# The last attention and the final norm of a two-block model, rescheduled on one core

## The reference

```python
proj = h @ w_in + b_in                      # h = rmsnorm(x, norm_c); q, k, v, g
logits = q k^T * scale - slope[head] * dist # 16 heads of 64, window 128, 2 kv heads
p = softmax([logits, sink])[..., :-1]       # dist >= 0 and dist < 128
o = p v
x = x + (o * silu(g)) @ w_out
return rmsnorm(x, final_norm)               # rows of 1024, one per token
```

## Time and profile before

| | us |
|---|---|
| median of 3 runs (1839.79 to 1842.37) | 1840.81 |
| the profiled execution | 1845.26 |
| its span | 1843.5 |
| from the start of the scores of head 0 to the start of the head loop's steady state | 1647.35 to 1668 |
| last values matmul to the eviction of the first residual tile | 1767.7 to 1784.96 |
| last residual tile taken out to the end | 1823.04 to 1843.5 |

### The profile page before, as it was taken

The page is one execution under the profiler, slowest core; times in us unless marked ns, Lnnn a source line. Parts: engine busy times, 40 slices in busy tenths (PEclk is TensorE's granted clock), DMA queues, the critical chain, the costliest instruction groups (busy, mean ns, idle before and its releaser), DMA issues.

```text
span 1843.5 us, 24067 instructions
## 1 busy us (share of the span) xinstructions
PE 1673.8 (91%) x8860; PEld 1412.3 (77%) x8860; DVE 1060.7 (58%) x1760; ACT 823.3 (45%) x1544; POOL 93.4 (5%) x112
## 2 busy tenths in 40 slices
PE   7998999998999999989999998889987979979977
PEld 6886787886778888868798896668765758859965
DVE  5557877674545656552254438864465984446654
ACT  5545665663334455541132226652353542235641
POOL 2000400000000000000000001100000100000001
PEclk9998999999999999999999999988997989989988
DMA  6411122113431333322223320111320111320011
GB/s 184 125 50 30 46 63 64 46 52 110 141 120 47 101 104 91 91 92 67 99 74 99 108 81 25 35 46 41 102 84 21 47 46 47 99 69 24 28 42 46
DMA packets 147870, 132.95 MB, mean 72 GB/s; under 512 B 8560, under 2 KB 142448, under 8 KB 147776
## 3 DMA queue, kind: packets, MB, share of 16 engines
q1 hardware_dynamic: 143744, 119.58, 21.3%
q0 software_dynamic: 3136, 10.78, 1.6%
q10 hardware_dynamic: 896, 1.32, 0.3%
HBM read 124.33 MB, written 7.34 MB: 71 GB/s over the span
## 4 chain that ended last, share of the span: by engine, by line
PE 74%; DVE 15%; ACT 5%; issue 5%; DMA 1%; DVEq 0%; ACTq 0%; POOL 0%
PE bank L292 19%; PE bank L293 19%; PE bank L294 19%; DVE wlo L285 2%; PE bank L1206 2%; PE bank L1220 2%; ACT whi L278 1%; PE bank L1189 1%; PE bank L2911 1%; DVE ptl L1374 1%; DVE sz L2700 1%; PE bank L2870 1%; PE bank L1223 1%; PE bank L2278 1%; PE bank L2883 1%
## 5 line engine op out<-in xcount | busy, mean ns | idle before, releaser
L292 PE MATMUL bank<-hh,whi 128*128 128x512 f32 (+3 forms) x1208 | 466.2, 386 | 16.0 <-DVE wlo L285 5.6
L293 PE MATMUL bank<-hl,whi 128*128 128x512 f32 (+3 forms) x1208 | 455.7, 377 | 0.0
L294 PE MATMUL bank<-hh,wlo 128*128 128x512 f32 (+3 forms) x1208 | 455.2, 377 | 0.0
L278 ACT ACTIVATE whi<-wraw 128x2048 fp32r<-128x2048 f32 x111 | 212.1, 1913 | 338.6 <-PE bank L294 338.5
L285 DVE TENSOR_TENSOR wlo<-wraw,whi 128x2048 fp32r<-128x2048 f32 x111 | 254.1, 2289 | 178.7 <-ACT whi L278 177.3
L292 PEld LDWEIGHTS bank<-hh,whi 128*128 128x128 f32 (+2 forms) x1208 | 231.2, 191 | 60.9 <-issue 5.8
L294 PEld LDWEIGHTS bank<-hh,wlo 128*128 128x128 f32 (+2 forms) x1208 | 230.5, 191 | 43.3
L293 PEld LDWEIGHTS bank<-hl,whi 128*128 128x128 f32 (+2 forms) x1208 | 231.2, 191 | 39.1 <-issue 0.7
L1374 DVE TENSOR_TENSOR ptl<-bank,pth 128x128 fp32r<-128x128 f32 (+3 forms) x128 | 56.8, 485 | 64.4 <-ACT pth L1282 63.0
L292 PE MATMUL bank<-ah,whi 128*128 128x512 f32 (+1 forms) x224 | 83.8, 374 | 10.6 <-DVE al L3046 8.3
L292 PE MATMUL bank<-yh,whi 128*128 128x512 f32 (+1 forms) x220 | 79.3, 360 | 6.7 <-DVE yl L1740 6.7
(11 more groups left out here) (393 smaller groups left out, 3212.2 us busy)
## 6 DMA issues: line engine op xcount, KB each, us to landing
wraw<-in_w_in_a_dram SPq DMA_DIRECT2D x52, 512.0 KB, 4.5
wraw<-in_w_up_dram SPq DMA_DIRECT2D x42, 512.0 KB, 4.9
wraw<-in_w_in_dram SPq DMA_DIRECT2D x34, 512.0 KB, 4.8
wraw<-in_w_in_c_dram SPq DMA_DIRECT2D x18, 512.0 KB, 4.7
wraw<-in_w_down_dram SPq DMA_DIRECT2D x16, 512.0 KB, 4.0
wraw<-in_w_out_a_dram SPq DMA_DIRECT2D x16, 512.0 KB, 4.0
aside<-stage POOLq DMA_DIRECT2D x20, 256.0 KB, 2.3
wraw<-in_w_attn_br_dram SPq DMA_DIRECT2D x8, 512.0 KB, 4.0
```

The source lines that it names most:

```text
L278: act.activation(whi[:, p], wraw[:, p], ACT.Copy).then_inc(w_hi_done, 1)
L292: pe.matmul(out, ws[0], hs[0], start=first, stop=False)
L293: pe.matmul(out, ws[0], hs[1], start=False, stop=False)
L294: return pe.matmul(out, ws[1], hs[0], start=False, stop=last)
```

## The change

It rewrites everything from the second half of the queries on; the code ahead is the same but for a few semaphores that are replaced by waits on existing counters.

1. The four late query tiles move into `window_attention`, and PE's order at its start is: query tiles 0 and 1, scores of head 0, query tile 2, scores of head 1, query tile 3, half a gate tile, then the head loop. They use banks 6, 7, 4 and 5.
2. Values and turned softmax are each split into a high and a low part (`vph3`, `vpl3`; `pth3`, `ptl3`), and `values` makes three one-pass matmuls for each float32 one. ACT now copies both turned banks (`high`), DVE subtracts (`low`), and `values` waits for DVE alone.
3. The diagonal matrices of the slopes are made on POOL. For heads whose slope is a power of two (every second one) the low part is zero, and its matmul is left out.
4. Silu, product, rounding and low part of the gates go pair by pair, in part ahead of the last head's work: ACT applies silu to four tiles before `high(15)`. The split of the second output weight item moves behind the gates on ACT and DVE.
5. `residual` and `final_norm` become `final_rows`: tile k-1 of the new x is transposed after the matmuls of tile k, squared with a row sum on ACT, multiplied by the norm weight on DVE into rows, and the last two tiles go in two halves of 256 tokens. The norm weight comes as a broadcast transfer of 512 KB (`wrow`), which SP issues behind the four weight loads, and DVE waits for it ahead of its first residual addition. The last scaling by the inverse root is shared by DVE and ACT.

```diff
+            act.wait_ge(drained, m0 + 2)
+            for g in range(2):
+                act.activation(vph3[:, :, HD + P * g:P + P * g], v3[:, :, HD * g:HD * g + HD], ACT.Copy) \
+                    .then_inc(v3_high, 1)
...
-            dve.tensor_scalar(nsink[:, :], pcol("sinks", n=NH), -1.0, None, ALU.mult).then_inc(ns_done, 1)
+            dve.tensor_tensor(v3[:, :, :], bank[1][:, :].rearrange("p (t d) -> p t d", t=TT),
+                              bv3[:, :].unsqueeze(1).to_broadcast([P, TT, P]), ALU.add).then_inc(drained, 1)
+            for g in range(2):
+                cols = slice(HD + P * g, P + P * g)
+                dve.wait_ge(v3_high, g + 1)
+                dve.tensor_tensor(vpl3[:, :, cols], v3[:, :, HD * g:HD * g + HD], vph3[:, :, cols].bitcast(F32),
+                                  ALU.subtract).then_inc(v3_low, 1)
+            dch(dve, dve.tensor_scalar(nsink[:, :], pcol("sinks", n=NH), -1.0, None, ALU.mult))
...
+        b0, d0 = new_items(2), new_tiles(4)
...
+        PROJ = (6, 7, 4, 5)
...
+        def exact(h):
+            return high_part(sl[h]) == sl[h]
         @block.sync
         def _(sp):
+            for j in range(2):
+                load_item(sp, b0 + j, 0, full_item(b0 + j, w["w_in_c_2"], 0, 2 * IC + IC * j))
             with sp.Fori(0, 2) as i:
...
+        @block.gpsimd
+        def _(pool):
+            for h in range(NH):
+                if h >= 2:
+                    pool.wait_ge(s_done, SD3 + 4 * (h - 1))
+                hi_ = high_part(sl[h])
+                ins = pool.tensor_scalar(dg3[:, h % 2, 0, :], ident[:, :], hi_, 1.0, ALU.mult, ALU.mult)
+                if not exact(h):
+                    ins = pool.tensor_scalar(dg3[:, h % 2, 1, :], ident[:, :], sl[h] - hi_, 1.0, ALU.mult, ALU.mult)
+                ins.then_inc(dg3_done, 1)
...
-                    pe.matmul(out, dg3[:, h % 2, 0, :], dist3[:, lo:2 * P], start=False, stop=False)
-                    pe.matmul(out, dg3[:, h % 2, 1, :], dist3[:, lo:2 * P], start=False, stop=True).then_inc(s_done, 1)
+                    mm = pe.matmul(out, dg3[:, h % 2, 0, :], dist3[:, lo:2 * P], start=False, stop=exact(h))
+                    if not exact(h):
+                        mm = pe.matmul(out, dg3[:, h % 2, 1, :], dist3[:, lo:2 * P], start=False, stop=True)
+                    mm.then_inc(s_done, 1)
...
-                pe.wait_ge(t3_act, h + 1)
-                pe.wait_ge(t3_dve, h + 1)
+                pe.wait_ge(t3_dve, 2 * h + 2)
...
-                    mm = pe.matmul(bank[6][:, P * j:P * j + n], vp3[:, j, c0:c0 + P],
-                                   pt3[:, h % 2, 2 * P * j:2 * P * j + n], start=(e == 0 and j == 0),
-                                   stop=(e == 1 and j == TT - 1), skip_group_check=True)
+                    for v, p in ((vph3, pth3), (vpl3, pth3), (vph3, ptl3)):
+                        mm = pe.matmul(bank[6][:, P * j:P * j + n], v[:, j, c0:c0 + P],
+                                       p[:, h % 2, 2 * P * j:2 * P * j + n],
+                                       start=(e == 0 and j == 0 and v is vph3 and p is pth3),
+                                       stop=(e == 1 and j == TT - 1 and p is ptl3), skip_group_check=True)
                 mm.then_inc(pv_done, 1)
...
+            def query_tile(t):
+                if t % 2 == 0:
+                    item_ready(pe, b0 + t // 2)
+                tile_of(pe, b0 + t // 2, t % 2, bank[PROJ[t]][:, :], H).then_inc(tiles, 1)
+            pe.wait_ge(drained, d0)
+            query_tile(0)
+            query_tile(1)
+            pe.wait_ge(c4_ready, 1)
+            pe.wait_ge(kd_low, 10)
+            pe.wait_ge(v3_pad, 1)
+            pe.wait_ge(v3_low, 2)
             scores(0)
-            for h in range(NH + 1):
-                if h:
-                    turn(h - 1)
+            query_tile(2)
+            scores(1)
+            query_tile(3)
+            gate_part(0)
+            for h in range(1, NH + 1):
+                turn(h - 1)
                 if h + 1 < NH:
                     scores(h + 1)
                 if h < NH:
                     gate_part(h)
-                if h:
-                    values(h - 1)
+                values(h - 1)
...
+            def high(v):
+                if v >= 2:
+                    act.wait_ge(pv_done, V3 + v - 1)
+                for b, c0, n in TURNED:
+                    act.wait_ge(t_done, T3 + 2 * v + b + 1)
+                    act.activation(pth3[:, v % 2, c0:c0 + n], bank[4 + b][:, 0:n], ACT.Copy).then_inc(t3_act, 1)
...
+            act.wait_ge(drained, d0 - 2)
             queries_high(0)
+            queries_high(1)
+            split_hi(act, n0)
+            expo(0)
+            expo(1)
+            split_hi(act, n0 + 1)
+            for h in range(1, NH):
+                if h >= 2:
+                    expo(h)
+                if h % 2 == 0:
+                    gate_out(h // 2 - 1)
+                high(h - 1)
                 if h % 2 and h >= 3:
                     out_pair(h // 2 - 1)
+                if h % 2 and h // 2 + 2 < NH // 2:
+                    queries_high(h // 2 + 2)
+                if h % 4 == 0:
+                    split_hi(act, n0 + h // 4 + 1)
+            for k in range(4):
+                silu(k)
+            high(NH - 1)
+            gate_out(KT - 1)
+            for k in range(4, KT):
+                silu(k)
+                gated_high(k - 4)
+            out_pair(KT - 1)
+            for k in range(4, KT):
+                gated_high(k)
+            split_hi(act, n0 + 5)
...
+            def low(v):
+                if v >= 2:
+                    dve.wait_ge(pv_done, V3 + v - 1)
+                for b, c0, n in TURNED:
+                    dve.wait_ge(t3_act, 2 * v + b + 1)
+                    dve.tensor_tensor(ptl3[:, v % 2, c0:c0 + n], bank[4 + b][:, 0:n],
+                                      pth3[:, v % 2, c0:c0 + n].bitcast(F32), ALU.subtract).then_inc(t3_dve, 1)
...
             queries_low(0)
+            query_out(0)
+            query_out(1)
+            split_lo(dve, n0)
+            maxima(0)
+            queries_low(1)
+            query_out(2)
+            maxima(1)
+            scaled(0)
+            query_out(3)
+            split_lo(dve, n0 + 1)
+            for h in range(1, NH):
+                if h >= 2:
+                    maxima(h)
+                    scaled(h - 1)
                 if h % 2 == 0 and h // 2 + 1 < NH // 2:
                     queries_low(h // 2 + 1)
                 if h % 4 == 1 and h > 1:
                     split_lo(dve, n0 + h // 4 + 1)
+                low(h - 1)
+            scaled(NH - 1)
+            gated_prod(0)
+            gated_prod(1)
+            low(NH - 1)
+            gated_prod(2)
+            gated_prod(3)
+            gated_low(0)
+            for k in range(4, KT):
+                gated_prod(k)
+                gated_low(k - 3)
+            for k in range(KT - 3, KT):
+                gated_low(k)
+            split_lo(dve, n0 + 5)
+        return (e_low, AHEAD + q0)
...
+    def final_rows(mat, rhs, ready):
+        n0, m0 = new_items(4), new_tiles(KT)
+        c = at_norm
+        BLOCKS = [(k, 0, TT) for k in range(6)] + [(6, 0, 2), (7, 0, 2), (6, 2, 4), (7, 2, 4)]
+        HALF = ((2, 3), (0, 1))
+        @block.sync
+        def _(sp):
+            with sp.Fori(0, 2) as i:
+                for j in range(2):
+                    load_item(sp, n0 + j, i, full_item(n0 + j, mat, 0, IC * j + 2 * IC * i))
+            sp.wait_ge(tiles, 2 * n0)
+            sp.dma_start(wrow[:, :], bvc[:, P:P + D].to_broadcast([P, D])).then_inc(got_con, 16)
+            for t, ends in ((0, 1), (1, 1), (2, 2), (3, 2)):
+                sp.wait_ge(y_fin if t % 2 == 0 else x_w, ends)
+                sp.dma_start(out[P * t:P * t + P, :], orow[:, t, :]).then_inc(stored, 16)
+            sp.wait_ge(stored, 16 * TT)
+        @block.tensor
+        def _(pe):
+            def turn(n):
...
+                for t in range(t0, t1):
+                    mm = pe.transpose(bank[4 + n % 4][:, P * t:P * t + P], xt[:, k, P * t:P * t + P], ident[:, :])
+                mm.then_inc(y_turned, 1)
+            pe.wait_ge(drained, m0)
+            for k in range(6):
+                if k % 2 == 0:
+                    item_ready(pe, n0 + k // 2)
+                if k >= 4:
+                    pe.wait_ge(drained, m0 + k - 3)
+                tile_of(pe, n0 + k // 2, k % 2, bank[k % 4][:, :], rhs, ready=ready if k == 0 else None) \
+                    .then_inc(tiles, 1)
+                if k:
+                    turn(k - 1)
+            item_ready(pe, n0 + 3)
+            pe.wait_ge(drained, m0 + 4)
+            half_tile(pe, n0 + 3, 0, bank[2], rhs, 0).then_inc(half_tiles, 1)
+            turn(5)
+            half_tile(pe, n0 + 3, 1, bank[3], rhs, 0).then_inc(half_tiles, 1)
+            turn(6)
+            pe.wait_ge(drained, m0 + 6)
+            half_tile(pe, n0 + 3, 0, bank[0], rhs, 1).then_inc(tiles, 1)
```

(128 more changed lines are left out.)

250 lines of the change are left out of this document (70 added, 180 removed).

## The result

The changed kernel takes 1815.09 us (median of 4 runs, 1809.34 to 1818.87) against 1840.3 beside it (1839.73 to 1842.37): ratio 0.9858, 95% interval 0.9831 to 0.9886. That is 25.2 us less, where 30.8 were forecast (1840.81 to 1810); it lies within the range. The profiled execution took 1818.87 us with a span of 1817.1.

What follows compares the result with a forecast made beforehand. PE was taken to bound the head loop, with waits and latency chains around it. The terms -18.85 - 9.65 + 9.55 - 12.15 = -31.1 us gave 1814.2 from the profiled 1845.26, 1810 against the median; range 1802 to 1820.

Steps and rivals of the forecast that it cites:

- The front: Late query tiles: interleaving covers PE waits of 5.89 and 3.35 us and slow stretches; one new wait of 0.8 us.
- The head loop: 16 heads, bound by PE: 6.79 or 6.32 us a head, 104.9 us in all, values matmuls 1.40 us.
- The bound by something else than columns: Values step: short matmuls not held by columns, so 1.40 us for 1.52, a gain of 0.12; columns alone 1.12.
- POOL beside DVE: Head loop: POOL's diagonals slow DVE by 0.1 to 0.45 us a head; 0 to 4 us, 0 taken.
- The last head: Head 15: ACT's table load and silus delay its softmax, PE idle 1.8 us; values end at 1748.85, minus 18.85.
- The gates: From the end of the last values to the first residual tile out: 7.6 us for 17.25, minus 9.65.
- The residual: Late norm weight: PE idle 3.85 us, slow clock 2.2, transposes 3.0, half tiles 0.5; plus 9.55.
- Rival (a): Residual: norm weight there in time, no stall or slow clock; 6.05 us less, 1804; chance 0.2.
- rival (b): Head loop paced by DVE, 7.2 us a head for 6.56; ten more, 1820; chance 0.12.
- (c): Head loop: PE falls idle in every head and its clock sinks; 9.8 us a head, 1862; chance 0.03.
- The end: From the last residual matmul to the end of the span: 8.3 us for 20.46, minus 12.15.

Runs made afterwards that it cites:

- front_old: Changed kernel with the old front order: all four late query tiles, then the scores of heads 0 and 1; 1825.12 us, ratio 0.9894 to the kernel before.
- gates_behind: Changed kernel with the four early silus behind the last head and the last output pair's copy ahead of all silus; 1818.84 us, ratio 0.9873 to the kernel before.
- wrow_early: Changed kernel with the norm weight transfer issued ahead of the fourth weight load; 1805.21 us, ratio 0.9786 to the kernel before.
- Again: The changed kernel, unaltered, timed again beside the kernel before; 1813.32 us, ratio 0.9834.
- tail_old: Changed attention with the residual and final norm of the kernel before in place of final_rows; 1812.32 us, ratio 0.9826 to the kernel before.

## Why the prediction came out as it did

In the four terms of the sum, measured from the landmark (before, after, change, forecast):

| | before | after | change | forecast |
|---|---|---|---|---|
| to the end of the values of head 15 | 171.5 | 153.3 | -18.2 | -18.85 |
| to the end of the first residual tile | 17.2 | 7.1 | -10.1 | -9.65 |
| to the last residual matmul | 38.1 | 48.8 | +10.7 | +9.55 |
| to the end of the span | 20.5 | 8.4 | -12.1 | -12.15 |
| sum | 247.3 | 217.6 | -29.7 | -31.1 |

The ends after are 1752.8, 1759.9, 1808.7 and 1817.1 in the profile.

**The front** was right, mechanism and size: 13.7 us by front_old, PE's own waits as read from the earlier trace rows, and a wait of 0.94 where 0.8 was put.

**The head loop** was right: 6.28 and 6.75 us where 6.32 and 6.79 stood. The values matmuls take 1.34 us, not 1.40. (The 0.79 us of the turn in the chain is no loss: the chain of the kernel before has 0.77 for the same seven transposes, and 0.68 is the distance of two starts.) The bound by something else than columns held: the expected 0.12 us a head measured 0.155.

**POOL beside DVE** cost the loop nothing, but the case the prediction feared did not arise there. A diagonal takes POOL 0.30 us, at the low end of the bounds. In the steady loop it always ran beside the maxima of DVE, which read banks and take 0.69 us with it, 0.68 without, and never beside an instruction that reads two operands from SBUF, such as the addition of 0.990 us in the earlier trace rows. Where it did meet one, POOL paid, as the last section shows.

**The last head** was a little too cheap: PE waited 1.80 us, as forecast, but then worked at the lower clock for the values and the first matmuls behind them (2.3 us for 1.4), which I had charged only to waits of 3.35 us and more. These 0.9 us are more than the 0.65 us missing in the first term. The lower clock did not come at the same place in every execution (last section), so part of this is chance.

**The gates** were right to half a microsecond, 7.1 us for 7.6. gates_behind shows that the early silus and the place of the last copy together are worth 6.0 us.

**The residual** was right in what I think the step worth learning: a transfer put behind a wait on SP that had moved. PE waited 3.95 us for the 3.85 forecast, and the next tile took 7.65 us (1770.26 to 1777.91) for 5.44, the 2.2 forecast. The mechanism is shown; that the size came out within 0.1 us is luck. The term mis-sized is the transfer: from the end of DVE's weight split, which frees the buffer, to its landing it took 7.4 us (1761.35 to 1768.73) for 6.04 in my sum, of which 5.83 for 4.9 fall behind its own issue. Against it, the split ended 8.5 us behind the last values for 10.1 in my sum, since ACT was through the gates sooner, and the second residual tile 12.7 for 13.05: 1.35 - 1.55 + 0.3 leaves 0.1. In the six other executions with the late transfer in front of the additions the transfer took 5.4 to 6.2 us from its issue and PE waited 3.17 to 4.66, so 3.85 is a typical size and not an exact one. Of the 1.1 us that the whole term lacked, 0.3 are the first transposes, which ran at half clock (0.77 us for 0.44), and another 0.3 the other transposes, 0.11 us each in the chain for 0.68/7; the rest is spread in parts too small to name. Rival (a), no stall, is the run wrow_early; rival (b), a loop paced by DVE, and (c) did not occur.

**The end** came out at 8.4 us for 8.3 by two misses that cancel. The last rows were scaled 4.4 us behind the last residual matmul (1808.7 to 1813.1) for 5.05, and the stores then took 4.0 us to the end of the span for 2.7 + 0.4. (The parts as written, 5.05 + 2.7 + 0.4, make 8.15, not 8.3.)

**The time**: the sum missed by 1.4 us, the profiled execution by 4.7 (1818.87 for 1814.2) and the median by 5.1. In the profiled execution the other 3.3 us lie ahead of the changed part; in the untraced ones it is not known where they lie. "Again" came to -29.3 us against the runs of the kernel before beside it, so a good part of the difference between 25.2 and 30.8 is scatter of the executions.

The parts add up when the stretch is divided at the last values. Ahead of them the kernel before took 169.7 us and the changed one 150.9, 18.8 less. The runs give front 14.0, slopes 3.8 and values 2.2, together 20.0; the wait ahead of the last values, which grew from 0.87 to 1.80 us, takes 0.9 back, which leaves 0.3. From there to the end it is 77.6 against 66.9, 10.6 less. gates_behind accounts for 6.4 of these and tail_old for 1.4 (of 8.4 that the new tail had in it). I did not separate the remaining 2.8; the pairwise order of the gates and the weight split that moved behind them are what is left of the diff there. Nor did I put the diagonals back on ACT by themselves.

## What to carry to other kernels

A wait belongs in front of the first instruction that reads the data, and a transfer in front of any wait in its queue that it does not need: the two placements here together cost 7 us, most of the 8.4 that the new tail had to give, and mending either one brought them back. When independent matmuls lie anywhere near a latency chain, put the chain between them; the idle time saved (8.7 us) returned about half as much again in clock (5 us). To compare parts of a long kernel, measure from a landmark just ahead of the change.

## What the runs showed that I had not expected

The same code ahead of the changed part ends anywhere between 1589.87 and 1600.51 us in twelve executions, so that the kernel's time spreads by more than half a percent between its own runs. The two extremes have mean granted clocks of 0.969 and 0.961 over the span. Whether the clock is the cause was not tried.

The lower clock came behind an idle time of 1.80 us too. In the kernel after it came 0.5 us into the last values (first window below), in "again", behind the same wait of 1.81 us, only behind the values, which so took 1.7 us and not 2.3 (second window).

```profile
1751.00:1754.00 3.00, 3.00 (x13) 2.81 (x13) 3.00 (x7) 3.00 (x6) 0.00 (x0) 0.50 0.00 0
```

```profile
1746.00:1749.00 3.00, 2.80 (x14) 2.31 (x13) 3.00 (x6) 3.00 (x6) 0.00 (x0) 0.64 0.00 0
```

POOL's op of 0.30 us twice took about 2 us in the kernel after (timeline of POOL):

```profile
1601.17 1.91 POOL L2866 TENSOR_SCALAR dg<-ident 128x128 fp32r<-128x128 f32 x1
1603.15 0.30 POOL L2868 TENSOR_SCALAR dg<-ident 128x128 fp32r<-128x128 f32 x1
...
1635.98 2.23 POOL L2868 TENSOR_SCALAR dg<-ident 128x128 fp32r<-128x128 f32 x1
```

Both times DVE was at a weight split, which reads two operands from SBUF (timeline of DVE):

```profile
1600.64 2.29 DVE L285 TENSOR_TENSOR wlo<-wraw,whi 128x2048 fp32r<-128x2048 f32 x1 [1.26 <-ACT whi L278]
...
1635.70 2.36 DVE L285 TENSOR_TENSOR wlo<-wraw,whi 128x2048 fp32r<-128x2048 f32 x1 [1.25 <-ACT whi L278]
```

The two operations of POOL ended 0.15 us behind the splits. The same pairs, with 1.91 and 2.23 us, stand beside a split in the traces of all other runs of the changed kernel but front_old. In front_old the split of the second pair is done before POOL starts, and there only the first operation is long, 1.91 us. So it is DVE's split that holds POOL, for its whole length, while the split itself grew by 0.07 us at most. Here nobody waited for the diagonals.
